# A hybrid decoder layer on one core: operand loads ahead of weight pieces on the load queue, gate rows requested later, fewer weight pieces per product and one copy moved to ScalarE

## What is computed

```python
h = rmsnorm(x, g_pre)
p = h @ w_in + b_in            # q_a k_a v_a z_a | q_m k_m v_m o_m z_m | i_m f_m | g_a g_b
att = sink_attention(window 128, 16 heads, 4 kv heads, rotary)     # branch A
hm  = mlstm(q_m, k_m, v_m, i_m, f_m)       # branch B: 4 heads of 256, chunks of 128, state C, n, m
y_a = att * silu(z_a);  y_m = sigmoid(o_m) * hm * silu(z_m)
merged = sigmoid(g_a) * (y_a @ w_pa) + sigmoid(g_b) * (y_m @ w_pb)
x = x + rmsnorm(merged @ w_out, g_post)
```

## Time and profile before

| what | value |
| --- | --- |
| median of 3 runs | 2826.03 us (2825.18 to 2828.23) |
| profiled execution | 2831.79 us, span of the trace 2830.0 us |
| TensorE, VectorE, ScalarE, GpSimd busy | 97%, 58%, 33%, 25% of the span |
| moved by DMA | 697.47 MB, mean 246 GB/s |
| granted TensorE clock, mean | 0.988 |

### The profile page before, as it was taken

How to read it: one execution, slowest core, us unless ns; L and a number is a source line. 1 busy time by engine, 2 the same in 40 slices (tenths; PEclk the granted TensorE clock), 3 DMA queues, 4 the chain that set the end, 5 groups by cost and what they waited for, 6 DMA issues and landing times. The chain is left out here.

```text
span 2830.0 us, 46426 instructions
## 1 busy us (share of the span) xinstructions
PE 2735.1 (97%) x15620; PEld 2287.2 (81%) x15620; DVE 1642.1 (58%) x4145; ACT 939.0 (33%) x2291; POOL 702.4 (25%) x1022
## 2 busy tenths in 40 slices
PE   6999999999999999999999999999999999999898
PEld 5888888888887867787887887888887888788786
DVE  5776665555663245465556546556337662577887
ACT  5774443444441021132122113114123231333533
POOL 3333533533551022202212222221100000022222
PEclk9999999999999999999999999999999999999999
DMA  8664566555767898888889888898896577957634
GB/s 316 236 219 159 173 200 208 170 181 168 228 221 259 280 339 279 289 271 291 292 270 301 283 283 292 265 291 279 290 328 218 197 266 248 325 191 242 212 149 149
DMA packets 410526, 697.47 MB, mean 246 GB/s; under 512 B 31778, under 2 KB 177575, under 8 KB 410260
## 3 DMA queue, kind: packets, MB, share of 16 engines
q1 hardware_dynamic: 298724, 526.72, 56.2%
q10 hardware_dynamic: 108848, 158.46, 16.4%
q0 software_dynamic: 2720, 9.32, 1.0%
HBM read 526.87 MB, written 169.48 MB: 246 GB/s over the span
## 5 line engine op out<-in xcount | busy, mean ns | idle before, releaser
L2847 PE MATMUL bank_second<-w_all,a_all 128*128 128x512 f32 x736 | 299.7, 407 | 12.2 <-DMA a_all<-hh_t 8.3
L2850 PE MATMUL bank_second<-w_all,a_all 128*128 128x512 f32 x736 | 289.5, 393 | 0.0
L2849 PE MATMUL bank_second<-w_all,a_all 128*128 128x512 f32 x736 | 288.9, 392 | 0.0
L2430 ACT ACTIVATE mx_qkt<-st_bank_t 128x512 f32<-128x512 f32 x68 | 40.8, 600 | 570.8 <-PE st_bank_t L2870 562.7
L2847 PE MATMUL bank_first<-w_all,a_all 128*128 128x512 f32 x496 | 200.2, 404 | 11.7 <-DMA a_all<-hh_t 3.9
L2850 PE MATMUL bank_first<-w_all,a_all 128*128 128x512 f32 x496 | 195.1, 393 | 0.0
L2849 PE MATMUL bank_first<-w_all,a_all 128*128 128x512 f32 x496 | 194.5, 392 | 0.0
L2847 PE MATMUL bank_third<-w_all,a_all 128*128 128x512 f32 x464 | 188.5, 406 | 4.3 <-DMA a_all<-sh_t 3.0
L308 PE MATMUL bank_first<-w_all,a_all 128*128 128x384 f32 x536 | 186.5, 348 | 0.0
L2850 PE MATMUL bank_third<-w_all,a_all 128*128 128x512 f32 x464 | 181.2, 390 | 0.0
L2849 PE MATMUL bank_third<-w_all,a_all 128*128 128x512 f32 x464 | 180.8, 390 | 0.0
(11 more groups left out here) (404 smaller groups left out, 7251.0 us busy)
## 6 DMA issues: line engine op xcount, KB each, us to landing
a_all<-sh_t SPq DMA_DIRECT2D x224, 512.0 KB, 5.4
a_all<-hh_t SPq DMA_DIRECT2D x180, 512.0 KB, 5.7
a_all<-hh_t ACTq DMA_DIRECT2D x104, 512.0 KB, 4.9
h_raw<-l_blocks_in ACTq DMA_DIRECT2D x64, 512.0 KB, 5.9
difs_t<-h_raw ACTq DMA_DIRECT2D x64, 512.0 KB, 6.6
st_waiting<-difs_t SPq DMA_DIRECT2D x118, 256.0 KB, 6.5
st_waiting<-l_blocks_in SPq DMA_DIRECT2D x84, 256.0 KB, 6.2
hh_t<-a_all SPq DMA_DIRECT2D x34, 512.0 KB, 6.0
```

Of the source, the lines that this page charges most:

```text
L2847: T.matmul(bank_view(bank, at), hi, weight_row(k, at, 0, t), start=fresh and t == 0, stop=False, skip_group_check=True)
L2849: T.matmul(bank_view(bank, at), hi, weight_row(k, at, 1, t), start=False, stop=False, skip_group_check=True)
L2850: last = T.matmul(bank_view(bank, at), lo, weight_row(k, at, 0, t), start=False, stop=t == KH - 1, skip_group_check=True)
```

## The change

It does five things. SyncE's loop issues the operand of q + 3 ahead of the pieces of step q. A tile's z and rows are requested two products ahead of its turning instead of four. The pieces of OUT are split 2.5 per product instead of 3, so their lowering and the loads of the later ones move back by up to one product. The copy of product 4 of a pair in OUT is done by ScalarE. And `amask` counts on `order_in`, for which VectorE now waits for three transfers, while TensorE's wait for `c_in` is for three instead of four.

```diff
--- before.py
+++ after.py
@@ -632,7 +632,7 @@
             load_xt(2)
             store_h(0)
             sp.dma_start(smask[:, :, :], k.c_smask).then_inc(order_in, 16)
-            sp.dma_start(amask[:, :, :], k.c_amask).then_inc(c_in, 16)
+            sp.dma_start(amask[:, :, :], k.c_amask).then_inc(order_in, 16)
             sp.dma_start(perm[:, :, :, :], k.c_perm).then_inc(order_in, 16)
             load_x(3)
             store_h(1)
@@ -1274,7 +1274,7 @@
             def sample_masks(a):
 
                 n0, d0 = PE_N * a, DVE_N * a
-                dve.wait_ge(order_in, 16 * 2)
+                dve.wait_ge(order_in, 16 * 3)
                 for i in range(2):
                     dve.wait_ge(smp_pe, n0 + 2 + i)
                     V.tensor_tensor_reduce(out=ssm[:, i, :], in0=p_s[i][:, 0:3 * P], in1=smask[:, i, :], scale=1.0,
@@ -1426,7 +1426,7 @@
             first_block(p_b[:, 0:W + GATES], attn_base(0) + ZC, W + GATES, k.AT[0] + 2, lambda: pe.wait_ge(gate_lo, 1)).then_inc(proj_b, 1)
             first_block(p_a[:, 0:ZC], attn_base(0), ZC, k.AT[0] + 5, lambda: scale_row(1)).then_inc(proj_a, 1)
             scale_row(2)
-            pe.wait_ge(c_in, 16 * 4)
+            pe.wait_ge(c_in, 16 * 3)
             T.matmul(p_s[1][:, 0:KVH], headrow, sink4[:, :], start=True, stop=True).then_inc(sink_done, 1)
 
             def gate_transposed(m):
@@ -1781,7 +1781,7 @@
     s, x = v // N_UNIT, v % N_UNIT
     if s == 0:
         return -3 if x < EARLY + KH else 5 + (x - EARLY - KH) // 2
-    return N_PROD * s - 6 + (x // 3 if s >= PA else x // 2)
+    return N_PROD * s - 6 + (x * 2 // 5 if s == OUT else x // 3 if s >= PA else x // 2)
 
 
 def unit_lowered_at(v):
@@ -2156,7 +2156,7 @@
                     sp.dma_start(lmask[:, :, :], k.c_lmask).then_inc(const_in[0], 16)
                     sp.dma_start(seqpair[:, :], k.c_seqpair).then_inc(const_in[1], 16)
                     load_states(0)
-                n = TURN.get(q + 4)
+                n = TURN.get(q + 2)
                 if n is not None:
                     load_z(n)
                     if n >= 2:
@@ -2193,10 +2193,10 @@
                     sp.dma_start(k.o_p_n[0, 0], nrow[NB * MH:, :]).then_inc(state_out, 16)
 
             for q in range(-4, Q_ALL + 8):
+                if 6 <= q + LOADED_AHEAD < Q_ALL:
+                    next_operand(q + LOADED_AHEAD)
                 for v in LOADS_AT.get(q, ()):
                     load_unit(v)
-                if 6 <= q + LOADED_AHEAD < Q_ALL:
-                    next_operand(q + LOADED_AHEAD)
                 if q < 0:
                     continue
                 s, x = q // N_PROD, q % N_PROD
@@ -2476,6 +2476,10 @@
                         act.wait_ge(prod, q)
                         act.wait_ge(c21_ready, m)
                         A.activation(t1[:, :], bank_x[:, :], ACT.Copy).then_inc(t1_ready, 1)
+                    if i and j == P2 and s == OUT:
+                        act.wait_ge(prod, q)
+                        wait_line(act, N_ITEM * s + i, 0, 0)
+                        A.activation(c[:, 0, 0:LW], bank_x[:, :], ACT.Copy).then_inc(c11_ready, 1)
                 if q + DIF_LEAD in DIF_NOW:
                     load_dif(DIF_NOW[q + DIF_LEAD])
                 if q - DIF_LEAD in DIF_NOW:
@@ -2586,9 +2590,7 @@
                     wait_line(dve, g, 0, 0)
                     if s in STREAMED:
                         V.tensor_tensor(c[:, 0, 0:LW], bank_x[:, :], bias_of(s)[:, 0:LW], ALU.add).then_inc(c11_ready, 1)
-                    elif s == OUT:
-                        V.tensor_copy(c[:, 0, 0:LW], bank_x[:, :]).then_inc(c11_ready, 1)
-                    else:
+                    elif s != OUT:
                         dve.wait_ge(e_in[0], 16 * row_turn(SCALING, g, 0))
                         V.scalar_tensor_tensor(out=c[:, 0, 0:LW], in0=e[:, 0, 0:LW], scalar=1.0, in1=bank_x[:, :],
                                                op0=ALU.add, op1=ALU.mult).then_inc(c11_ready, 1)
```

## The result

The change made the kernel slower. In four runs beside four of the kernel before, the median is 2849.28 us (2843.89 to 2852.86) against 2826.39 us: ratio 1.0085, 95% interval 1.0072 to 1.0098. (The ratio is not the quotient of the two medians, which is 1.0081.) Measured once more, with six runs beside ten of before (an eleventh, in the slow state at 3854 us, is left out), the ratio is 1.0072 (1.0052 to 1.0093). The forecast was 2820.0 us with a range up to 2829.

The account below looks back on a forecast made before the run. With matrix products at 97% of the span, only TensorE's idle time and slow-clock stretches could be won; the terms summed to -6.0 us, taking the median from 2826.03 to 2820.0 us, range 2808 to 2829.

Parts of the forecast that it names:

- GA to PA: Change of pass GA to PA: operand wait at GA/59 falls from 4.08 to 0.5 us, VectorE limits the gain; -2.8 us.
- GB to PB: Change of pass GB to PB: the 4.19 us wait shrinks, GpSimd's sum then holds VectorE; -0.6 us, bounds -6.3 and +1.
- ZM to H0: Change of pass ZM to H0: operand waits go, but H0/6's piece has one more operand ahead; +0.7 us.
- PA to GB: Change of pass PA to GB: three short operand waits, 0.9 us in all, each behind pieces; -0.7 us, bounds -1 and +1.
- H0/28: 28th product of pass H0: its operand lands 3 to 4 us sooner, removing the 3.26 us wait and slow clock; -4.7 us.
- product 36 of H0, H1, H2: Operand 36 of these head passes: 256 KB more of loads in front, 0.7 us each; +2.1 us, bounds 0 and +6.
- PB to OUT: Change of pass PB to OUT: OUT/4 and OUT/6 start earlier, moved pieces delay OUT/7; +1.0 us, bounds -7.7 and +3.
- masks: TensorE's first product with the sinks: part of its 3.30 us wait for an unread mask goes; -1.0 us, bounds -5 and 0.
- operands ahead of pieces: SyncE's queue at changes of pass: operand issued where the first weight piece stood; at GA/59 6.2 us earlier, -2.8 us booked.
- Rival (c): Head passes: later-requested rows and z hold up VectorE at early tiles, +9 us in sum, 2835; chance 0.13.
- Rival (a): Changes of pass and H0/28: the waits go whole, VectorE is no bound; 21.6 us won, 2804.4; chance 0.15.
- Rival (b): Changes of pass: order buys nothing, waits only move from operand to piece; 0 with +-3, 2826; chance 0.17.

Follow-up runs that it names:

- the swap alone: Kernel before, changed only so that a product's operand is issued ahead of its weight pieces; ratio 1.0042 (1.0030 to 1.0055).
- the wait alone: Kernel before, transfers in the old order, but SyncE waits for a free operand buffer ahead of the pieces; ratio 1.0022 (1.0010 to 1.0034).

## Why the prediction was wrong

The forecast had the right mechanism at several of its places, and left out the place of the largest loss. The measured numbers are the change less the kernel before, in single executions.

| term | forecast, us | measured |
| --- | --- | --- |
| GA to PA | -2.8 | GA/57 to PA/9: -5.2, though unchanged executions take up to 5.6 less than the profiled one |
| GB to PB | -0.6 | GB/57 to PB/9: +0.1 |
| ZM to H0 | +0.7 | +4.2; the swap alone +3.8 |
| H0 to H1, H1 to H2, H2 to H3 | no term | +10.6; the swap alone +8.6 |
| H3 to GA | no term | +1.1; the swap alone +1.2 |
| PA to GB | -0.7 | PA/57 to GB/9: +0.7; the swap alone -0.2 |
| H0/28 | -4.7 | -4.2; the rows alone -4.6 |
| product 36 of H0, H1, H2 | +2.1 | +4.9, +4.7, -2.2; the rows alone +4.0, +5.1, +0.2 |
| PB to OUT | +1.0 | +2.5; the pieces alone +2.0 |
| copy on ScalarE | 0 | 0 |
| masks | -1.0 | 0 (ratio 1.0000 +- 0.0010) |

**The step that failed** is "operands ahead of pieces", which was priced only where the earlier trace rows showed a wait to be won. The swap acts at every change of pass up to GB to PB, also at H0 to H1, H1 to H2, H2 to H3 and H3 to GA, where TensorE waited for nothing. The sum put these at nothing without a reason. There the swap had nothing to win and, as the runs show, only some 1.4 us of slack to lose; the pieces came 4.2 us late, and TensorE lost 8.6 us by the swap alone (10.6 in the change). The kernel of the swap alone is slower by 12 us, and the one that has it only from GA/12 on is not.

**Its price was wrong too.** For ZM to H0 the prediction counted what stands ahead of a piece in bytes, "one more operand ahead of it (512 KB, 1.3 us)". That part was near: 1.8 us at H1/6, and at ZM/50 to H0/10 itself the swap costs 1.3 us more than the wait alone (73.4 against 72.1). But the operand's issue includes a wait for a free buffer, and a piece behind it inherits the wait: 2.4 us at landing, 3.9 us at issue (1279.30 against 1274.74, each from the start of its H1/6), and 2.6 us of TensorE's time at ZM/50 to H0/10. The front section had named this wait. In the prediction it appears only as something that the operands suffer.

**Product 36** was the right place with a wrong size: 256 KB "are 0.7 us", measured 2.5 us (3.53 against 0.99), and a slower clock for the product behind it, twice. The bound of +6 for three took the clock in; with the rows alone +9.3 came. That counts H2 as +0.2, but its 15.7 us before lie above the 12.7 to 13.7 of five unchanged executions. Of the 2.5 us at H0/36, 1.3 are the later issue (1.0 of it the issue of the two loads and the gaps); 1.3 lie in the transfers and weren't taken apart.

**PB to OUT** came out near by two errors against each other. The start of OUT/4 was to come 1.8 us sooner and that of OUT/6 2.4. From the start of OUT they come after 14.4 and 22.5 us, where they came after 14.4 and 22.2. VectorE has three pieces fewer to lower there, but the three directly ahead of its copy st_c<-bank_first, beside a sum of GpSimd that begins at 2671.59 (L2292), take 1.8 us longer. First before, then after:

```profile
2656.13 1.89 DVE L2525 TENSOR_TENSOR w_all<-st_more_waiting,w_all 128x512 fp32r<-128x512 f32 x3
```

```profile
2671.44 3.69 DVE L2529 TENSOR_TENSOR w_all<-st_waiting,w_all 128x512 fp32r<-128x512 f32 x3
```

OUT/7, for which +3.4 us were added on top, starts only 1.6 us later, after 30.3 instead of 28.7 us, in all six executions with fewer pieces. (Some pieces of OUT move back by two products, not by up to one as said with the change: piece 20, counted from 0, is split at step 8 instead of 6.)

**The ends of GA and GB** were read nearly right, with VectorE's st_u at PA/7 (1.06 us) and the transposes at PB (3.00 us) as the new waits; no wait came at PA/4, and 1.32 us stayed at GB/59. The aim was smaller than it looked: the waits at GA/59 and GB/59, 4.08 and 4.19 us in the profile of before, lie between 0.92 and 4.10 and between 1.38 and 4.55 in seven other executions of the old order. The profiled execution of before, 5.8 us above the median, had both nearly at their longest.

**Rival (c)** had a time of 2835 and a chance of 0.13. It was nearest in time, and by luck, for its reason was another: it let VectorE wait for late rows at tile 0. The rows alone leave the starts of H1 to H3 at 134.9 us against 134.3. Late were the pieces, through ScalarE's queue. Rival (a) fell at PA/7 and at PB, where waits for VectorE and GpSimd came. Rival (b), order buys nothing, describes the ends best: net 0.9995 for the swap there.

## What to carry to other kernels

When an issue is moved ahead of others in a queue, list everything that it passes at every place where the loop runs, not only where a wait is to be won, and count its own wait with it: what it passes inherits that wait, and this can be more than its bytes. A place without a wait isn't free: read its slack, here ScalarE's 1.82 us of idle time before the copy of the transposed q and k, and what is queued behind the operation that comes late. Before a burst of slow issues every small load is dear; move such loads around it. And read a wait in several executions before it becomes a term of a sum.

## What was not expected of the hardware

A wait for another engine brought the low clock as one for a DMA does. The prediction allowed for it at PB, and the kernel before shows it already: after the 3.56 us for VectorE's st_u at 2673.12 the clock is 0.64. In the change, after the 3.00 us for GpSimd's sum at 2499.33 the granted clock is 0.50 (1.2 GHz), and in the stretch with the 5.00 us for VectorE's st_u it is 0.53. The first row is of before, the others of the change:

```profile
2673.10:2677.90 4.80, 4.78 (x14) 3.79 (x15) 2.88 (x5) 0.39 (x1) 2.38 (x1) 0.64 0.09 32
...
2499.20:2502.60 3.40, 3.27 (x12) 2.98 (x13) 3.37 (x6) 0.00 (x0) 0.66 (x2) 0.50 0.98 371
...
2690.00:2697.00 7.00, 5.22 (x12) 4.13 (x13) 4.20 (x7) 0.00 (x0) 2.38 (x1) 0.53 0.05 19
```

The Trainium skill (TensorE: Matmul & The Clock Gate, Loop structure matters more than you think) sets the copy of a result out of PSUM beside the matmuls, as work that doesn't cool TensorE. Its example has the next matmuls follow at once. Here TensorE has to wait for such an eviction, and these rows show the lower clock.
